# A two-layer decoder trunk on one core: three more projection pairs as split products, rotary angles on GpSimd

## The chip, the cores and the metric

The kernel runs on one core of one Trainium2 chip. The metric is device time in microseconds: 1081.44 us is the median of three runs of the kernel before (1079.23 to 1082.0).

## The reference

Two layers (D = 1024, 256 positions, batch 1) over a residual x, and a last RMSNorm. Each layer's first half, cut to what matters:

```
h = rmsnorm(x, norm1_g[l]) * (1 + sc1) + sh1          # shifts and scales from silu(c) @ w_mod
z = h @ w_in[l]                                       # one wide projection
ya = rglru_branch(...z...)                            # convolution, gated linear recurrence
yb = diff_attention(zq, zk, zv, positions, ...)       # ang = positions * inv_freq; cos, sin; partial rotary
yc = rwkv7_mix(...z...)                               # token shift, LoRA products, state recurrence
merged = sigmoid(za)*(ya@Wa) + sigmoid(zb)*(yb@Wb) + sigmoid(zc)*(yc@Wc)
x = x + gt1 * (merged @ w_out[l])
```

In `rwkv7_mix` the token shift is z_t + (z_{t-1} - z_t) * mu, and three small LoRA products give decay, `a` and gate: tanh(wd) @ w2, ad @ a2, sigmoid(gd) @ g2. The second half of a layer is a gated MLP with a short convolution. All of it is fp32, and so is the output.

## The kernel before

Everything lies in SBUF with channels on partitions: X, H and the projected tiles are 128 channels x 256 positions. The engines run five streams of instructions written out by hand; semaphores alone set their order, and each engine works its queue strictly in order.

**Pairs.** The large weights come as pairs of output tiles, 1 MB each (two halves of 128x1024), in a ring of four slots. SyncE issues pair g when pair g - 4 is done (`pair`, L500). In a layer, pair 0 is the LoRA inputs, 1 and 2 are K, 3 and 4 R, 5 and 6 V, 7 to 10 the recurrent branch (`LR` = 7), 11 to 16 the attention's q, k, v (`AT` = 11), and the gates and merges follow (`GA` = 17).

**Plain and split products.** A pair is multiplied in one of two ways. `product` (L1826) is 16 plain fp32 matmuls a pair (the trace lists each as two). `product_split` takes three reduced-width (fp32r) matmuls for each plain one: high weight x high input, high x low, low x high (`passes`, L1806 to L1808). It needs the high part of the weights, a ScalarE copy (`half_pairs_high`, L702, into WC or WCR, alternating by pair), the low part, a VectorE subtraction (`half_pairs_low`, L1198, written over the ring slot as RLO), and the same for the input: `input_high` (L688, L689, into HG0 and HG1) and `input_low` (L1212, HGL over H). HG0 lies over SW, where the first layer's LoRA weights are too. Layer 1 is split from pair 1 on; layer 0 from pair 7 (`split_from`). The first split pair of a layer does its two products on the high input first and the one on the low input after them.

**Order around the change, layer 0.** TensorE: pairs 0 to 3, the products that sum the shift of the first pairs (`shift_column`, L1814, inside pair 2, on the sums GG that VectorE accumulates at L1184 and L1187), the LoRA products for decay and `a` (L1897, waiting for ScalarE's tanh, L720 to L723), pairs 4 and 5, the LoRA gate product (L1907), pairs 6, 7, 8, the kk sums (L1926), pairs 9 and 10, the bonus sums (L1937), pairs 11 to 16. ScalarE: evacuations of each pair (`evac`, L672; L821 for pairs 11 on), the tanh block between the evacuations of pairs 2 and 3, then some derived values, the two sines (L733, L734), the LoRA tanhs (L740), and the high parts. VectorE: token shift of the LoRA inputs, two `wmod` blocks, `derived` (lambda terms, and the rotary angles L1057 to L1076: positions times frequency, then the range reduction, once for sine and once for cosine; last the sine's sign, L1101), the shift of K (L1156 to L1160), scans and shifts of R and V, and the low parts between them; from L1394 on the rotation with SIN and COS. GpSimd: memsets, the DMAs of later `wmod` blocks (L570), two kinds of additions later on, and nothing else in this stretch.

Of the kernel before, what the change touches and what calls it, by code (L numbers as in the profile page):

```python
# [23 lines left out]
I32 = mybir.dt.int32  # L24
# [134 lines left out]
FILL_ZY = 6  # L159
FILL_TURN, FILL_READ, FILL_CHAIN, FILL_STATE, FILL_OUT = 4, 8, 4, 6, 8  # L160
# [36 lines left out]
def trunk_kernel(nc, wmain, wmod, small, v1v2, params, consts, lqk, x_t, positions, y_t):  # L197
    ctx = ExitStack()
    with ctx:
# [154 lines left out]
        def split_from(l):  # L354

            return 1 if l else LR

        def lora_weights(l, a, n):

            return (R[:, 8:12, :].rearrange("p a b -> p (a b)") if l else SW)[:, a:a + n]  # L360
# [115 lines left out]
        def _(sp):  # L476
# [37 lines left out]
            for l in range(L):  # L514
# [7 lines left out]
                if l == 0:  # L522
                    sp.dma_start(lora_weights(l, WL, 1024), small[l, :, 0:1024]).then_inc(s_sw, 16)
# [34 lines left out]
        def _(pool):  # L558
# [13 lines left out]
            def add_squares(n):  # L572

                pool.wait_ge(x_sq, 8 * n + 4)
                pool.tensor_tensor(H[:, 0:2, :], H[:, 0:2, :], H[:, 2:4, :], ALU.add).then_inc(sq_add, 1)
                pool.wait_ge(sq_add, 4 * n - 3)
# [3 lines left out]
                pool.wait_ge(sq_add, 4 * n - 1)  # L580
                pool.tensor_tensor(H[:, 0, :], H[:, 0, :], H[:, 4, :], ALU.add).then_inc(sq_add, 1)

            pool.wait_ge(s_w[2], 16)
            for l in range(L):
# [7 lines left out]
                m1 = m0 + 16  # L592
                mod_blocks(m0 + 2, m1)
# [30 lines left out]
        def _(act):  # L624
# [49 lines left out]
            for l in range(L):  # L674
# [16 lines left out]
                def half_pairs_high(a, b):  # L691

                    for y in range(a, b):
                        k, m = LR + y // 2, y % 2
                        g, far = PAIRS * l + k, k >= split_from(l) + 2
                        if m == 0:
                            act.wait_ge(s_w[g % 4], 16 * (g // 4 + 1))
                        if far and m == 0:
                            act.wait_ge(p_half, (GA - LR) * l + k - 2 - split_from(l) + 1)
# [17 lines left out]
                evac(l, 2, G[:, 4:6, :])  # L717
                next_high(2)
# [7 lines left out]
                if l == 0:  # L726
# [19 lines left out]
                for b in range(2):  # L746
                    A(GG[:, 2 * b:2 * b + 2, :], duo(4 + b), ACT.Copy).then_inc(lora_act, 1)
                if l == 0:
                    input_high()
                    half_pairs_high(0, 4)  # L750
                else:
                    next_high(5)
                evac(l, 6, G[:, 12:14, :])
                if l:
                    next_high(6)
# [270 lines left out]
        def _(dve):  # L1026
# [16 lines left out]
            def derived():  # L1043
# [12 lines left out]
                ang, k1, red = YB[:, 2, :], YB[:, 3, :], RT[:, :]  # L1056
                V.tensor_copy(YB[:, 1, :], YB[:, 0, :].bitcast(I32)).then_inc(step, tick(n_step))  # L1057
                after()
                V.tensor_scalar(ang, YB[:, 1, :], C[:, FREQ:FREQ + 1], None, ALU.mult).then_inc(step, tick(n_step))
                for n, out in enumerate((red, YB[:, 1, :])):  # L1060
                    after()
                    V.tensor_scalar(k1, ang, 1.0 / SQ2PI, 0.25 * n, ALU.mult, ALU.add).then_inc(step, tick(n_step))
                    after()
                    V.tensor_scalar(k1, k1, MAGIC, None, ALU.add).then_inc(step, tick(n_step))
                    after()
                    V.tensor_scalar(k1, k1, -MAGIC, None, ALU.add).then_inc(step, tick(n_step))
                    after()
                    V.scalar_tensor_tensor(out, k1, -C1, ang, ALU.mult, ALU.add).then_inc(step, tick(n_step))
                    after()
                    V.scalar_tensor_tensor(out, k1, -C2, out, ALU.mult, ALU.add).then_inc(step, tick(n_step))  # L1070
                    after()
                    V.scalar_tensor_tensor(out, k1, -C3, out, ALU.mult, ALU.add).then_inc(step, tick(n_step))
                    after()
                    V.tensor_scalar(out, out, 0.5 * math.pi * n, PI_IN, ALU.add, ALU.min).then_inc(step, tick(n_step))
                    after()
                    V.tensor_scalar(out, out, -PI_IN, None, ALU.max).then_inc(pre_dve, 1)  # L1076
# [19 lines left out]
                V.reduce_sum(sm[:, 24:25], mat(ROT), AX_X).then_inc(step, tick(n_step))  # L1096
                after()
                V.tensor_scalar(sm[:, 24:25], sm[:, 24:25], -1.0, None, ALU.mult).then_inc(step, tick(n_step))
                after()
                dve.wait_ge(pre_act, 6)  # L1100
                V.tensor_scalar(SIN[:, :], SIN[:, :], sm[:, 24:25], None, ALU.mult).then_inc(step, tick(n_step))  # L1101
# [64 lines left out]
            for l in range(L):  # L1166
# [25 lines left out]
                def half_pairs_low(a, b):  # L1192

                    for y in range(a, b):
                        s = (PAIRS * l + LR + y // 2) % 4
                        part = slice(y % 2 * D, y % 2 * D + D)
                        dve.wait_ge(ph_ready, 2 * (GA - LR) * l + 2 * (LR - split_from(l)) + y + 1)
# [39 lines left out]
                early_low(4)  # L1237
                after()
# [4 lines left out]
                early_low(5)  # L1243
                dve.wait_ge(lora_act, 10 * l + 8)
# [34 lines left out]
                if l == 0:  # L1279
                    half_pairs_low(0, 2)  # L1280
                    input_low()
# [103 lines left out]

                for b in range(4):
# [345 lines left out]
        def _(pe):  # L1732
# [44 lines left out]
            def ones_sum(n, between=None):  # L1777
                for m in range(KT) if n == 0 else (0, 6, 7):
                    if n and m == 0:
                        pe.wait_ge(sq_add, 4 * n)  # L1780
# [54 lines left out]
            def product_split(l, k):  # L1835
# [4 lines left out]
                for m in range(2):  # L1840
                    pe.wait_ge(pl_ready, 2 * (GA - LR) * l + y1 + m + 1)
# [22 lines left out]
            for l in range(L):  # L1864
# [35 lines left out]
                for k in (4, 5):  # L1900
                    if l:
                        product_split(l, k)
                    else:
                        product(l, k, H)
# [3 lines left out]
                last.then_inc(lora_mm, 1)  # L1908
                if l:
                    product_split(l, 6)  # L1910
                    product_split(l, LR)
# [5 lines left out]
                    product_split(l, LR + 1)  # L1917
                else:
                    product(l, 6, H)
                    product_split(l, LR)  # L1920
                    product_split(l, LR + 1)
# [517 lines left out]
```

## Time and profile before

| | |
|---|---|
| median of three runs | 1081.44 us |
| the profiled execution | 1079.48 us, its span 1077.9 us |
| TensorE busy | 1055.1 us, 98% |
| VectorE busy | 849.6 us, 79% |
| ScalarE busy | 582.2 us, 54% |
| GpSimd busy | 120.0 us, 11% |
| granted TensorE clock, mean | 0.996 |

Read the busy shares as averages over many stages. What a change is worth shows in the chain that ended last and in who waits for whom in the stretch that it touches, here the first 150 us.

### The profile page before, as it was taken

Reading aid. Unit: us, or ns where it says so; the run is one execution under the profiler, and the core shown is the slowest. Engines: PE = TensorE matmul, PEld = TensorE weight load, DVE = VectorE, ACT = ScalarE, POOL = GpSimd, SP = SyncE. Lnnn points to the kernel's source line nnn. Section 1 sums busy time; section 2 is a strip of 40 time slices with the busy share of each in tenths; the row PEclk is TensorE's granted clock in tenths of the full one; section 3 lists DMA queues with packets and bytes.
Section 4 is the critical chain, followed back from the end, with each engine's and each line's share of the span. In section 5 each row is a group of like instructions: output and inputs, shape, how many; then the busy total and the mean of one; then the engine's idle time right before and its main releaser. Section 6 shows DMA issues by size and latency. Waiting matters only on the chain.

```text
span 1077.9 us, 24053 instructions
## 1 busy us (share of the span) xinstructions
PE 1055.1 (98%) x10020; PEld 965.3 (90%) x10020; DVE 849.6 (79%) x1255; ACT 582.2 (54%) x894; POOL 120.0 (11%) x138
## 2 busy tenths in 40 slices
PE   7999999999999999999999999999999999999997
PEld 6789988788798999999989999878877999999996
DVE  5798998686687889987768899978766878888763
ACT  2266567632555666663455575783328466666433
POOL 0100000056002000001120000002530200000001
PEclk9999999999999999999999999999999999999999
DMA  9956445544246566668855546451615565455651
GB/s 368 345 197 227 172 167 227 194 158 139 99 181 253 212 234 228 229 225 293 319 168 195 196 162 230 159 204 65 231 61 195 185 245 195 175 178 192 227 204 40
DMA packets 41751, 214.86 MB, mean 199 GB/s; under 512 B 8096, under 2 KB 8736, under 8 KB 22336
## 3 DMA queue, kind: packets, MB, share of 16 engines
q1 hardware_dynamic: 30144, 171.65, 43.3%
q0 software_dynamic: 11520, 41.95, 11.1%
q8 instruction: 67, 1.10, 0.4%
q14 instruction: 20, 0.16, 0.0%
HBM read 212.01 MB, written 1.05 MB: 198 GB/s over the span
## 4 chain that ended last, share of the span: by engine, by line
PE 92%; DVE 3%; DMA 3%; SPq 1%; ACT 1%; issue 1%; DVEq 0%; ACTq 0%
PE ps L1808 18%; PE ps L1806 18%; PE ps L1807 18%; PE ps L1996 6%; PE ps L2000 6%; PE ps L1994 6%; PE ps L1826 4%; PE ps L2105 3%; DMA TK<-wmod_dram 2%; DVE macc L1119 1%; PE ps L2283 1%; PE ps L1764 1%; PE ps L2096 1%; DMA mring<-wmod_dram 1%; PE ps L2021 1%; PE ps L1951 1%
## 5 line engine op out<-in xcount | busy, mean ns | idle before, releaser
L972 ACT ACTIVATE WH<-ring 128x1024 fp32r<-128x1024 f32 x144 | 151.9, 1060 | 163.9 <-PE ps L1808 155.8
L1650 DVE TENSOR_TENSOR WLO<-ring,WH 128x1024 fp32r<-128x1024 f32 x144 | 175.4, 1232 | 66.7 <-ACT WH L972 66.7
L1808 PE MATMUL ps<-HH,WLO 128*128 128x256 f32 x736 | 208.4, 283 | 0.0
L1807 PE MATMUL ps<-HL,WH 128*128 128x256 f32 x736 | 206.8, 281 | 0.0
L1806 PE MATMUL ps<-HH,WH 128*128 128x256 f32 x736 | 205.2, 279 | 0.0
L1808 PEld LDWEIGHTS ps<-HH,WLO 128*128 128x128 f32 x736 | 138.9, 189 | 0.0
L1806 PEld LDWEIGHTS ps<-HH,WH 128*128 128x128 f32 x736 | 138.7, 188 | 0.0
L1807 PEld LDWEIGHTS ps<-HL,WH 128*128 128x128 f32 x736 | 138.1, 188 | 0.0
L570 POOL DMA_DIRECT2D mring<-wmod_dram x80 | 43.2, 540 | 761.7 <-DVE macc L1119 456.0
L1119 DVE SCALAR_TENSOR_TENSOR macc<-mring,sm,macc 128x1024 f32<-128x1024 f32 x70 | 96.4, 1377 | 18.2 <-DMA mring<-wmod_dram 15.8
L1808 PE MATMUL ps<-GH,WLO 128*128 128x256 f32 x384 | 108.4, 282 | 0.0
L1806 PE MATMUL ps<-GH,WH 128*128 128x256 f32 x384 | 108.3, 282 | 0.0
L1807 PE MATMUL ps<-GL,WH 128*128 128x256 f32 x384 | 108.0, 281 | 0.0
L1808 PE MATMUL ps<-HG,RLO 128*128 128x256 f32 x384 | 108.0, 281 | 0.0
L1678 DVE SCALAR_TENSOR_TENSOR TK<-ps,PR,TK 128x255 f32<-128x255 f32 x192 | 79.1, 475 | 0.0
L2000 PE MATMUL ps<-RLO,HG 128*128 128x512 f32 x192 | 77.8, 405 | 0.0
L1808 PEld LDWEIGHTS ps<-GH,WLO 128*128 128x128 f32 x384 | 73.7, 192 | 0.0
L1808 PEld LDWEIGHTS ps<-HG,RLO 128*128 128x128 f32 x384 | 72.6, 189 | 0.0
L1807 PEld LDWEIGHTS ps<-GL,WH 128*128 128x128 f32 x384 | 72.3, 188 | 0.0
L1806 PEld LDWEIGHTS ps<-GH,WH 128*128 128x128 f32 x384 | 72.1, 188 | 0.2
L785 ACT ACTIVATE WC<-ring 128x1024 fp32r<-128x1024 f32 x36 | 37.7, 1054 | 55.0 <-PE ps L1996 31.9
L1806 PE MATMUL ps<-HG,WCR 128*128 128x256 f32 x208 | 58.9, 283 | 0.0
(404 smaller groups left out, 2499.9 us busy)
## 6 DMA issues: line engine op xcount, KB each, us to landing
ring<-wmain_dram SPq DMA_DIRECT2D x150, 1024.0 KB, 4.9
mring<-wmod_dram POOLq DMA_DIRECT2D x80, 512.0 KB, 5.1
G<-wmod_dram SPq DMA_DIRECT2D x3, 1024.0 KB, 9.3
R<-wmod_dram SPq DMA_DIRECT2D x2, 1024.0 KB, 18.2
TK<-wmod_dram SPq DMA_DIRECT2D x2, 1024.0 KB, 19.8
X<-x_t_dram SPq DMA_DIRECT2D x1, 1024.0 KB, 4.9
R<-wmod_dram SPq DMA_DIRECT2D x2, 512.0 KB, 12.2
y_dram<-H SPq DMA_DIRECT2D x4, 256.0 KB, 2.2
```

The costliest lines, as they stand in the source:

```text
L570: pool.dma_start(mring[:, n % 2, :], wmod[mod_row(n)]).then_inc(s_m[n % 2], 16)
L972: A(WH[:, n % 2, part], ring[:, b, part], ACT.Copy).then_inc(hi_ready, 1)
L1119: V.scalar_tensor_tensor(macc[:, u % 2, :], block, sm[:, CSIL + kt:CSIL + kt + 1], macc[:, u % 2, :], ALU.mult, ALU.add).then_inc(mod_used, 1)
L1650: V.tensor_tensor(WLO[:, n % 2, part], ring[:, b, part], WH[:, n % 2, part].bitcast(F32), ALU.subtract).then_inc(lo_ready, 1)
L1678: ins = V.scalar_tensor_tensor(UB[:, q % 2, t, d:S], duo(b)[:, t, 0:S - d], PR[:, l, bass.ds(j + (COL["fw"] + 48 * (2 - d)), 1)], UB[:, q ...
L1806: MM(out, w_high[:, at], high, start=start, stop=False, skip_group_check=True)
L1807: MM(out, w_high[:, at], low, start=False, stop=False, skip_group_check=True)
L1808: return MM(out, w_low[:, at], high, start=False, stop=stop, skip_group_check=True)
L1826: last = MM(ps[:, g % 4, m * S:(m + 1) * S], w_of(g, m, i), rhs[:, i, :], start=(i == 0), stop=(i == KT - 1))
L1994: MM(ps[:, b, :], high[:, tk], w_high, start=(k == 0), stop=False, skip_group_check=True)
L1996: i = MM(ps[:, b, :], low[:, tk], w_high, start=False, stop=False, skip_group_check=True)
L2000: i = MM(ps[:, b, :], high[:, tk], w_low, start=False, stop=(k == nk - 1), skip_group_check=True)
```

## The change

It does four things, all in layer 0:

1. `split_from(0)` is 4 instead of 7: pairs 4, 5 and 6 are split products. `input_high` and the high parts of pairs 4 to 8 move forward in ScalarE's queue (the first two right behind the evacuation of pair 2), and `input_low` and the low parts of pairs 4 to 7 in VectorE's (`early_low`).
2. The first layer's LoRA weights w2, a2, g2 go to R[:, 8:12], as the second layer's do, since HG0 is now written while they are in use. SyncE waits for nine used `wmod` blocks ahead of that load.
3. The rotary angles are computed by GpSimd, in 24 instructions (VectorE's fused multiply-adds become a multiply and an addition), after its memset of R and ahead of its further `wmod` DMAs. `derived` is cut in three: `derived`, `derived_mid` and `sine_signed`.
4. ScalarE takes the sines after the high parts of pair 8, and VectorE puts the sine's sign in ahead of the first rotation.

```diff
         def split_from(l):
-            return 1 if l else LR
+            return 1 if l else 4
         def lora_weights(l, a, n):
-            return (R[:, 8:12, :].rearrange("p a b -> p (a b)") if l else SW)[:, a:a + n]
+            return R[:, 8:12, :].rearrange("p a b -> p (a b)")[:, a:a + n]
...
                 if l == 0:
+                    sp.wait_ge(mod_used, added(9))
                     sp.dma_start(lora_weights(l, WL, 1024), small[l, :, 0:1024]).then_inc(s_sw, 16)
...
+            def angles():
+                pool.wait_ge(s_par, 64)
+                pool.wait_ge(h_pre, 8)
+                ang, k1, red = YB[:, 2, :], YB[:, 3, :], RT[:, :]
+                pool.tensor_copy(YB[:, 1, :], YB[:, 0, :].bitcast(I32)).then_inc(sq_add, 1)
+                pool.wait_ge(sq_add, 1)
+                pool.tensor_scalar(ang, YB[:, 1, :], C[:, FREQ:FREQ + 1], None, ALU.mult).then_inc(sq_add, 1)
+                for n, out in enumerate((red, YB[:, 1, :])):
+                    done = 2 + 11 * n
+                    pool.wait_ge(sq_add, done)
+                    pool.tensor_scalar(k1, ang, 1.0 / SQ2PI, 0.25 * n, ALU.mult, ALU.add).then_inc(sq_add, 1)
+                    pool.wait_ge(sq_add, done + 1)
+                    pool.tensor_scalar(k1, k1, MAGIC, None, ALU.add).then_inc(sq_add, 1)
+                    pool.wait_ge(sq_add, done + 2)
+                    pool.tensor_scalar(k1, k1, -MAGIC, None, ALU.add).then_inc(sq_add, 1)
+                    for i, part in enumerate((C1, C2, C3)):
+                        pool.wait_ge(sq_add, done + 3 + 2 * i)
+                        pool.tensor_scalar(COS[:, :], k1, -part, None, ALU.mult).then_inc(sq_add, 1)
+                        pool.wait_ge(sq_add, done + 4 + 2 * i)
+                        pool.tensor_tensor(out, COS[:, :], ang if i == 0 else out, ALU.add).then_inc(sq_add, 1)
+                    pool.wait_ge(sq_add, done + 9)
+                    pool.tensor_scalar(out, out, 0.5 * math.pi * n, PI_IN, ALU.add, ALU.min).then_inc(sq_add, 1)
+                    pool.wait_ge(sq_add, done + 10)
+                    pool.tensor_scalar(out, out, -PI_IN, None, ALU.max).then_inc(sq_add, 1)
...
                 def next_high(k):
-                    if l:
+                    if k + 2 >= split_from(l):
                         half_pairs_high(2 * (k + 2 - LR), 2 * (k + 3 - LR))
...
                 evac(l, 2, G[:, 4:6, :])
+                if l == 0:
+                    input_high()
                 next_high(2)
                 act.wait_ge(lora_z, 2 * l + 2)
                 A(YA[0:64, 0, :], YA[0:64, 0, :], ACT.Tanh).then_inc(lora_t, 1)
...
-                    act.wait_ge(pre_dve, 5)
-                    A(SIN[:, :], RT[:, :], ACT.Sin).then_inc(pre_act, 1)
-                    A(COS[:, :], YB[:, 1, :], ACT.Sin).then_inc(pre_act, 1)
...
+                next_high(5)
+                evac(l, 6, G[:, 12:14, :])
+                next_high(6)
                 if l == 0:
-                    input_high()
-                    half_pairs_high(0, 4)
+                    act.wait_ge(sq_add, TRIG)
+                    A(SIN[:, :], RT[:, :], ACT.Sin).then_inc(pre_act, 1)
+                    A(COS[:, :], YB[:, 1, :], ACT.Sin).then_inc(pre_act, 1)
...
                 def early_low(k):
-                    if l:
+                    if k >= split_from(l):
                         half_pairs_low(2 * (k - LR), 2 * (k + 1 - LR))
...
                 shift(G[:, 2:6, :], K_, 4, l, 2)
                 early_low(4)
+                if l == 0:
+                    input_low()
...
                 early_low(5)
+                if l == 0:
+                    derived_mid()
...
                 if l == 0:
-                    half_pairs_low(0, 2)
-                    input_low()
                     half_pairs_low(2, 4)
...
+                if l == 0:
+                    sine_signed()
                 for b in range(4):
...
                 for k in (4, 5):
-                    if l:
-                        product_split(l, k)
-                    else:
-                        product(l, k, H)
+                    product_split(l, k)
```

The angle instructions that `derived` loses (L1057 to L1076), and the counts of the semaphores that go with the longer list of split pairs, are left out here.

## Rows read from the trace of the kernel before

**Rows 1.** The page's first part: busy us, share of the span, instructions.
```profile
PE 1055.1 (98%) x10020; PEld 965.3 (90%) x10020; DVE 849.6 (79%) x1255; ACT 582.2 (54%) x894; POOL 120.0 (11%) x138
```

**Rows 2.** The chain that ended last, 38 to 150 us: start, us, what.
```profile
45.82 0.79 PE ps L1814 x8
46.60 7.45 PE ps L1826 x34
...
56.94 14.01 PE ps L1826 x64
...
72.68 6.91 PE ps L1826 x32
```

**Rows 3.** ScalarE's timeline: start, us, what, idle before and its releaser.
```profile
48.97 1.28 ACT L720 ACT_TABLE_LOAD   x1
...
51.02 0.42 ACT L723 ACTIVATE YA<-YA 128x256 f32<-128x256 f32 x1
...
75.58 2.00 ACT L702 ACTIVATE WC<-ring 128x1024 fp32r<-128x1024 f32 x2
...
122.82 0.60 ACT L821 ACTIVATE R<-ps 128x512 f32<-128x512 f32 x1 [3.20 <-PE ps L1808]
...
128.50 0.60 ACT L821 ACTIVATE R<-ps 128x512 f32<-128x512 f32 x1 [3.18 <-PE ps L1808]
```

**Rows 4.** The tile `ring`, 46 to 52 us: loads of pairs 4 to 6.
```profile
L500 SPq DMA_DIRECT2D ring<-wmain_dram x3: 430/430/513, 47.0 to 48.0; - x3
...
DMA to landing us min/median/max: 5.0/7.7/11.0
```

**Rows 5.** The load of the positions (line L491).
```profile
L491 SPq DMA_DIRECT2D YB<-positions_dram x1: 1710/1710/1710, 24.5 to 24.5; - x1
...
DMA to landing us min/median/max: 14.9/14.9/14.9
```

**Rows 6.** VectorE's timeline, 38 to 130 us.
```profile
39.37 5.47 DVE L1187 SCALAR_TENSOR_TENSOR GG<-ring,mod,GG 128x512 f32<-128x512 f32 x7
...
47.77 0.69 DVE L1156 TENSOR_TENSOR YA<-G 128x510 f32<-128x510 f32 x1 [0.96 <-ACT G L682]
...
52.56 0.29 DVE L1057 CAST YB<-YB 128x256 f32<-128x256 int32 x1
...
59.07 0.15 DVE L1081 TENSOR_TENSOR sm<-sm 128x1 f32<-128x1 f32 x1
...
61.28 0.36 DVE L1101 TENSOR_SCALAR SIN<-SIN,sm 128x256 f32<-128x256 f32 x1
...
64.72 1.14 DVE L1240 TENSOR_SCALAR KK<-ZS,PR 128x256 f32<-128x256 f32 x4
...
76.74 2.36 DVE L1198 TENSOR_TENSOR RLO<-ring,WC 128x1024 fp32r<-128x1024 f32 x2 [0.32 <-ACT WC L702]
79.63 2.36 DVE L1212 TENSOR_TENSOR HGL<-H,HG 128x1024 fp32r<-128x1024 f32 x2 [0.53 <-PE ps L1826]
81.91 2.35 DVE L1198 TENSOR_TENSOR RLO<-ring,WCR 128x1024 fp32r<-128x1024 f32 x2
84.17 1.22 DVE L1156 TENSOR_TENSOR ZS<-G 128x1020 f32<-128x1020 f32 x1
...
105.76 1.29 DVE L1322 TENSOR_TENSOR BON<-ps,ZS 128x512 f32<-128x512 f32 x2 [0.75 <-PE ps L1937]
...
126.52 2.35 DVE L1198 TENSOR_TENSOR RLO<-ring,WC 128x1024 fp32r<-128x1024 f32 x2
```

**Rows 7.** GpSimd's instructions by form: count, busy us, mean ns, idle before.
```profile
L581 POOL TENSOR_TENSOR H<-H 128x256 f32<-128x256 f32 x4 | 2.9, 734 | 0.3
...
L559 POOL MEMSET SW<- 128x1024 f32 x1 | 1.0, 951 | 0.3 <-POOLq L2432 0.3
```

**Rows 8.** Timelines of GpSimd and VectorE, 326 to 336 us.
```profile
330.13 1.75 POOL L577 TENSOR_TENSOR H<-H 128x256 f32<-128x256 f32 x1
...
330.06 2.91 DVE L1650 TENSOR_TENSOR WLO<-ring,WH 128x1024 fp32r<-128x1024 f32 x2 [0.37 <-ACT WH L972]
```

More of the change, by code:

```diff
@@ L159 @@
 FILL_ZY = 6
+TRIG = 24
 FILL_TURN, FILL_READ, FILL_CHAIN, FILL_STATE, FILL_OUT = 4, 8, 4, 6, 8
@@ L575, in add_squares @@
                 pool.tensor_tensor(H[:, 0:2, :], H[:, 0:2, :], H[:, 2:4, :], ALU.add).then_inc(sq_add, 1)
-                pool.wait_ge(sq_add, 4 * n - 3)
+                pool.wait_ge(sq_add, TRIG + 4 * n - 3)
                 pool.tensor_tensor(H[:, 0, :], H[:, 0, :], H[:, 1, :], ALU.add).then_inc(sq_add, 1)
@@ L579, in add_squares @@
                 pool.tensor_tensor(H[:, 4, :], H[:, 4, :], H[:, 5, :], ALU.add).then_inc(sq_add, 1)
-                pool.wait_ge(sq_add, 4 * n - 1)
+                pool.wait_ge(sq_add, TRIG + 4 * n - 1)
                 pool.tensor_tensor(H[:, 0, :], H[:, 0, :], H[:, 4, :], ALU.add).then_inc(sq_add, 1)
+            def angles():
[22 more added lines that the diff above has]
+                    pool.tensor_scalar(out, out, -PI_IN, None, ALU.max).then_inc(sq_add, 1)
             pool.wait_ge(s_w[2], 16)
@@ L592, in _ @@
                 m1 = m0 + 16
+                if l == 0:
+                    angles()
                 mod_blocks(m0 + 2, m1)
@@ L698, in half_pairs_high @@
                         if far and m == 0:
-                            act.wait_ge(p_half, (GA - LR) * l + k - 2 - split_from(l) + 1)
+                            act.wait_ge(p_half, (GA - split_from(0)) * l + k - 2 - split_from(l) + 1)
                         elif far:
@@ L1055, in derived, with derived_mid @@
                 V.scalar_tensor_tensor(CEN[:, :], mat(BLOCKS), -1.0 / 64, mat(IDENT), ALU.mult, ALU.add).then_inc(cen_ready, 1)
[L1056 to L1076, printed above, removed]
+            def derived_mid():
                 dve.wait_ge(pre_act, 4)
@@ L1095, in derived, with sine_signed @@
                 after()
-                V.reduce_sum(sm[:, 24:25], mat(ROT), AX_X).then_inc(step, tick(n_step))
+                V.reduce_sum(sm[:, CSH:CSH + 1], mat(ROT), AX_X).then_inc(step, tick(n_step))
                 after()
-                V.tensor_scalar(sm[:, 24:25], sm[:, 24:25], -1.0, None, ALU.mult).then_inc(step, tick(n_step))
+                V.tensor_scalar(sm[:, CSH:CSH + 1], sm[:, CSH:CSH + 1], -1.0, None, ALU.mult).then_inc(step, tick(n_step))
+            def sine_signed():
                 after()
                 dve.wait_ge(pre_act, 6)
-                V.tensor_scalar(SIN[:, :], SIN[:, :], sm[:, 24:25], None, ALU.mult).then_inc(step, tick(n_step))
+                V.tensor_scalar(SIN[:, :], SIN[:, :], sm[:, CSH:CSH + 1], None, ALU.mult).then_inc(step, tick(n_step))
                 after()
@@ L1196, in half_pairs_low @@
                         part = slice(y % 2 * D, y % 2 * D + D)
-                        dve.wait_ge(ph_ready, 2 * (GA - LR) * l + 2 * (LR - split_from(l)) + y + 1)
+                        dve.wait_ge(ph_ready, 2 * (GA - split_from(0)) * l + 2 * (LR - split_from(l)) + y + 1)
                         V.tensor_tensor(RLO[:, s, part], ring[:, s, part], half_high(y).bitcast(F32), ALU.subtract).then_inc(pl_ready, 1)
                 def early_low(k):
-                    if l:
+                    if k >= split_from(l):
                         half_pairs_low(2 * (k - LR), 2 * (k + 1 - LR))
@@ L1384, in dve_chunks @@
                         weights_low(x)
+                if l == 0:
+                    sine_signed()
                 for b in range(4):
@@ L1779, in ones_sum @@
                     if n and m == 0:
-                        pe.wait_ge(sq_add, 4 * n)
+                        pe.wait_ge(sq_add, TRIG + 4 * n)
                     else:
@@ L1840, in product_split @@
                 for m in range(2):
-                    pe.wait_ge(pl_ready, 2 * (GA - LR) * l + y1 + m + 1)
+                    pe.wait_ge(pl_ready, 2 * (GA - split_from(0)) * l + y1 + m + 1)
                     out, wh, wl = ps[:, g % 4, m * S:(m + 1) * S], half_high(y0 + m), RLO[:, g % 4, m * D:m * D + D]
@@ L1900, in _ @@
                 for k in (4, 5):
-                    if l:
-                        product_split(l, k)
-                    else:
-                        product(l, k, H)
+                    product_split(l, k)
                 pe.wait_ge(lora_act, 10 * l + 4)
@@ L1908, in _ @@
                 last.then_inc(lora_mm, 1)
+                product_split(l, 6)
+                product_split(l, LR)
                 if l:
-                    product_split(l, 6)
-                    product_split(l, LR)
                     pe.wait_ge(lora_act, 10 * l + 8)
@@ L1916, in _ @@
                     last.then_inc(zv_up, 1)
[L1917 to L1921, printed above, removed]
+                product_split(l, LR + 1)
                 pe.wait_ge(kk_sq, l + 1)
```

3 lines of the change are left out of this document (removed).

## The prediction

> **What bounds the kernel now.** I read the page first: TensorE is busy for 98% of the span [rows 1], so a change pays only through TensorE's own work or its waits. Next, the chain that ended last, from 46 to 80 us [rows 2]: it lies on TensorE alone. Pair 3 ends at 54.05; pairs 4 and 5, as plain fp32 products, take 14.01 us together, pair 6 takes 6.91. The reader is to see that nothing else is on that chain there. Then ScalarE's timeline [rows 3]: pairs 13 and 14 are split products, and their evacuations start 5.68 us apart, so a split pair costs 5.68 us. Last, VectorE's timeline [rows 6]: it runs the low parts of the weights just ahead of TensorE. The low part of pair 15 starts at 126.52, its first half (half of 2.35 us) is there at 127.7, and TensorE takes pair 15 shortly before 128.50, when the evacuation of pair 14 begins [rows 3]. I take 0.6 us of room (0.8 at most). VectorE is the second bound.
>
> **The change, part by part.**
> *Pairs 4 to 6 split.* TensorE's work falls by 14.01 + 6.91 - 3 x 5.68 = 3.9 us.
>
> *ScalarE ahead of the LoRA tanh.* `input_high` (two copies) and the high parts of pair 4 (two more) now stand in ScalarE's queue before the tanh that TensorE's LoRA products wait for. A copy of that shape takes 1.0 us (two take 2.00) [rows 3]. The tanh's table load began at 48.97; after `input_high` ScalarE is free at 50.9, but pair 4 isn't there: it is issued at 47.0 and the quickest of the three issues needs 5.0 us [rows 4], so 52.0. Two copies to 54.0, then the old stretch from table load to the last copy, 51.44 - 48.97 = 2.5 us [rows 3]: 56.4. TensorE is there at 54.05 and loses 2.4 us. Behind it wait the evacuation of pair 3 and all later ones. Net for TensorE alone: 3.9 - 2.4 = 1.5 us gained.
>
> *LoRA weights in R[8:12].* One load moves in its destination only. SyncE issues it after a wait for nine blocks, which VectorE finishes before SyncE comes to that point; what is queued behind it, the other small weights, the masks and pair 4, isn't held. Cost 0.
>
> *Low parts and derived vectors on VectorE.* The old way from the angles' first instruction to the shift of V is 52.56 to 84.17. Out go the angles, 52.56 to 59.07, 6.5 us, the sine's sign (0.36, with its wait 0.4) and two idle gaps of 0.32 and 0.53, which were waits for ScalarE's late high parts and for pair 6 [rows 6]. In come three more pairs of low parts at 84.17 - 81.91 = 2.26 us, 6.8 us. Sum -6.5 - 0.4 - 0.85 + 6.8 = -1.0: without anything else VectorE would come to the shift of V 1.0 us earlier. It wins another 0.75 at the bonus, where it waited for TensorE, and gives 0.4 back where the sine's sign now stands, ahead of the first rotation [rows 6].
>
> *Angles on GpSimd.* 24 instructions on 128x256: 18 with one input tensor, 6 with two. They begin at 24.5 + 14.9 = 39.4, when the positions land [rows 5]. The sines are wanted by ScalarE only at about 80, so their own length costs nothing, nor does the delay of the `wmod` blocks queued behind them on GpSimd (used from 91 us). But GpSimd and VectorE hold each other up: at 330.06 two VectorE instructions with both inputs in SBUF take 2.91 us beside GpSimd additions [rows 8], against 2.35 for two of the same form and shape at 81.91 with GpSimd idle [rows 6]. In between ran one 128x256 addition of GpSimd, which took 1.75 us instead of its 0.73 [rows 7, 8]. So one two-input instruction of GpSimd costs VectorE 0.55 us, and they take turns. The one-input instruction isn't in this trace. Below, a memset of 128x1024 takes 0.95 [rows 7], a quarter of it 0.24; above, the two-input 0.55. I take 0.3, about half of the two-input one, since it reads half as much.
>
> How much of this is covered: VectorE's seven accumulations end at 39.37 + 5.47 = 44.84 [rows 6], and TensorE's product on their result starts at 45.82 [rows 2], so they may be about 0.8 us late with a signal's way kept. They take turns with six one-input instructions, 6 x 0.3 = 1.8 us: 1.0 uncovered, for TensorE at 46 and for VectorE behind it (TensorE gives it back, since the tanh stays at 56.4). While VectorE then waits for that product and for ScalarE (0.8 us and the 0.96 us before 47.77 [rows 2, 6]), three more fit, two of them two-input. Fifteen are left: 4 x 0.55 + 11 x 0.3 = 5.5 us, all before the shift of K ends, in a stretch where VectorE has no idle time. The delay in all, call it C, is 1.0 + 5.5 = 6.5. Ends: C = 0 if they don't hold each other up here; with 0.55 for all, 6 x 0.55 - 0.8 + 15 x 0.55 = 10.8.
>
> The Trainium skill (SBUF — State Buffer, Who interferes with whom) says that a VectorE instruction with two SBUF inputs, or in a two-port mode, and a GpSimd instruction that reads SBUF exclude each other for the whole instruction. By that rule, the trace agrees with its 0.55 us, all 24 instructions exclude VectorE. The skill (GPSIMD Engine Reference, Engine selection) calls GpSimd's one-input work roughly line rate; by VectorE's 0.96 GHz an estimate of 0.27 us for 256 columns, and C would be 6.0; no row here shows such an instruction.
>
> *The sum.* TensorE is ready for pair 4 at 56.4 plus the LoRA products, 56.94 - 54.05 = 2.9 [rows 2], 59.3. VectorE begins the shift of K at 52.56 instead of 61.67 (the sine's sign and 0.03); it takes until 64.72, 3.05 us [rows 6], half a low part 1.13, so 56.7 without C and about 63 with it. TensorE waits 3.9 us there, and doesn't get ahead again: by its own work it would start pair 8 at 59.3 + 4 x 5.68 + the gate products, 72.68 - (56.94 + 14.01) = 1.7 [rows 2], 83.7; the first half of that pair's low part stands 2.26 - 1.13 before the shift of V, 83.2 - 1.1 + 6.5 = 88.6. What remains at pair 15 is VectorE's lateness less the room: C - 1.0 - 0.75 + 0.4 - 0.6 = C - 1.95. With C = 6.5 that is +4.55 us. After it TensorE is ahead of nothing that would give it back: the scores' operands come with about 1.9 us of room, and from there TensorE is the bound. The profiled execution took 1079.48 us, so 1084.0; it stands 1.96 under the median of the runs, 1081.44, and the prediction is made on that: 1086.0.
>
> **Rivals.**
> *The two engines don't get in each other's way here* (C near 0, or under 1.95). TensorE's own sum decides: 1.5 us gained, 1079.9, not slower. For it: three quarters of GpSimd's instructions have one input, and the row that prices the conflict is of two inputs on both sides. Against: 1.75 for 0.73. It decides while C is under about 0.5; the sign turns at C = 1.95.
> *One-input instructions cost as much as two-input ones.* C = 10.8, +8.85 us, 1090.3; the accumulations would be 2.5 us late for TensorE's product at 46.
> *The tanh isn't late and VectorE keeps ahead.* Then 3.9 us of TensorE's work would come free; VectorE's lead limits it to 1.95, 1079.5. A gain of over 0.3% (3.2 us) needs both bounds to be wrong. ScalarE's queue order speaks against it.
> *Pair 4 lands later than 52.0* (the third of the three needs 11.0 us [rows 4]). Up to 3.9 us more are hidden by the wait for VectorE in my case; where C is near 0, 3 us more are a loss of 1.5 net, 1082.9: within no change.
>
> **Numbers.** Forecast case 0.5 (one-input price between 0.2 and 0.4: C from 4.8 to 8.2, +2.9 to +6.2). No conflict 0.25, with the late pair 4 in it. Full price 0.18. Clear gain 0.07. The range reaches from VectorE's bound on a gain, 1079.5, to the full price, 1090.3. 0.3%, about what a measurement can tell from no change, is 3.2 us; of the forecast case about 0.45 of 0.5 lies above it. Slower 0.45 + 0.18 = 0.63, same 0.25 + 0.05 = 0.3, faster 0.07.
>
> **What the profile after would show.** GpSimd's angle instructions at about 0.45 us each (hold and issue), from 39.4 to about 60, and stretched beside VectorE; VectorE's accumulations in GG, its shift of K and its first low parts lengthened by about 7 us together, some 0.8 of it without effect; the LoRA products at 56.4 instead of 54; TensorE idle for some 4 us before pair 4, with VectorE's RLO as releaser, and again by some tenths before pairs 5 to 8 and 15; the shift of V at about 89.7. If instead that shift starts near 83 and TensorE's only new gap is the 2.4 us at 54, the conflict was mis-sized and the time is near 1080. If GpSimd's one-input instructions take 0.7 us alone, the upper rival holds.

## The result, and the profile of the changed kernel

The changed kernel took 1087.54 us (median of 5 runs, 1085.92 to 1089.09) against 1081.44 us: 6.1 us slower, ratio 1.0063 with a 95% interval of 1.0048 to 1.0078. The forecast was 1086.0 us, slower. The profiled execution took 1087.13 us, its span is 1085.3 us, 7.4 us over that of before. The sign and most of the size came out, but in the trace only 2.3 of these 7.4 us arose where the forecast put the loss; the rest has another cause. One run of e1 below, 1149.24 us at a granted clock of 0.85, is a slow one and is left out of its figures.

The page's first part, after; before is [rows 1]:

```profile
PE 1052.5 (97%) x10068; PEld 963.1 (89%) x10068; DVE 854.6 (79%) x1243; ACT 589.2 (54%) x900; POOL 146.1 (13%) x162
```

TensorE has 48 matmuls more (three pairs of 48 in place of 32) and 2.6 us less work. GpSimd's busy time grew by 26 us for the 24 angle instructions; at the shortest time of each form, given below, they would take 18 x 0.40 + 6 x 0.73 = 11.6 us.

ScalarE's timeline, after (the copies ahead of the tanh) [rows 3]:

```profile
49.32 1.08 ACT L718 ACTIVATE HG<-H 128x1024 fp32r<-128x1024 f32 x1
50.27 1.08 ACT L719 ACTIVATE HG<-H 128x1024 fp32r<-128x1024 f32 x1
51.81 2.01 ACT L732 ACTIVATE WCR<-ring 128x1024 fp32r<-128x1024 f32 x2 [0.46 <-DMA ring<-wmain_dram]
53.84 1.28 ACT L752 ACT_TABLE_LOAD   x1
...
55.89 0.42 ACT L755 ACTIVATE YA<-YA 128x256 f32<-128x256 f32 x1
```

The last tanh copy ends at 56.3, and the LoRA products start at 56.51; the forecast said 56.4. TensorE's waits from 50 to 100 us, after:

```profile
PE ps L1824 <- DVE RLO L1212: 2.0, 2, 1.3
PE ps L1915 <- issue: 2.0, 1, 2.0
```

The second line is the wait for the tanh. The first is the wait for low parts, ahead of pairs 5 and 6. GpSimd's angle instructions by form, after (count, busy us, mean ns, idle before):

```profile
L603 POOL TENSOR_SCALAR COS<-YB 128x256 f32<-128x256 f32 x6 | 7.4, 1234 | 0.5
L605 POOL TENSOR_TENSOR YB<-COS,YB 128x256 f32<-128x256 f32 x3 | 3.0, 1003 | 0.3
...
L609 POOL TENSOR_SCALAR YB<-YB 128x256 f32<-128x256 f32 x1 | 1.9, 1902 | 0.1
```

The shortest one-input instruction takes 0.40 us and the shortest two-input one 0.73; beside VectorE most of them stretch to between 0.85 and 1.9 (1.09 on the mean of all 24). VectorE's timeline, after [rows 6]:

```profile
39.46 6.54 DVE L1201 SCALAR_TENSOR_TENSOR GG<-ring,mod,GG 128x512 f32<-128x512 f32 x7
...
57.28 3.09 DVE L1212 TENSOR_TENSOR RLO<-ring,WCR 128x1024 fp32r<-128x1024 f32 x2
60.30 3.09 DVE L1226 TENSOR_TENSOR HGL<-H,HG 128x1024 fp32r<-128x1024 f32 x2
63.31 1.99 DVE L1256 TENSOR_SCALAR KK<-ZS,PR 128x256 f32<-128x256 f32 x4
...
87.28 1.21 DVE L1170 TENSOR_TENSOR ZS<-G 128x1020 f32<-128x1020 f32 x1
```

The accumulations take 6.54 us for 5.47, a low part 3.09 for 2.35, KK 1.99 for 1.13: the two engines do hold each other up. The shift of V starts at 87.28. Without conflict the forecast had it at 83.2, so C, the delay by the conflict, is 4.1 us and not 6.5.

How late is each kernel at fixed points of the program? The table takes the start of the same VectorE instruction in each trace, less its start before. The first column is the scores, where the changed stage ends. Each row is one execution, set against one of the kernel before (1079.48 us, near the fastest of its runs), so a row says where time goes; what it is worth is told by the medians.

| profiled execution | 147.12 (scores) | 215.73 | 240.71 | 540.60 | 785.49 (layer 1) | 998.82 |
|---|---|---|---|---|---|---|
| after | +2.32 | +3.47 | +4.59 | +6.05 | +5.94 | +7.23 |
| only angles (e2) | +0.46 | -0.04 | +0.15 | +1.48 | +1.66 | +1.71 |
| tanh first, no angles (e7) | -1.99 | -1.06 | +0.01 | +1.37 | +1.25 | +2.57 |
| before, 48 matmuls more (e9) | +1.44 | +2.65 | +3.62 | +4.61 | +4.22 | +5.54 |
| after, 128 matmuls more (e11) | +2.04 | +1.62 | +2.14 | +2.29 | +2.29 | +2.29 |
| e7, 128 matmuls more (e10) | -2.31 | -2.73 | -2.21 | -2.01 | -2.13 | -2.17 |
| only pair 6 split (e12) | -0.79 | +1.67 | +2.10 | +3.31 | +3.42 | +3.44 |

("128 more" counts the 48 of the split pairs and 80 that do no work.) The changed stage costs 2.3 us. Another 3.7 us come between the scores and 541 us and 1.3 near 795 us, where the change has altered nothing. That part was the question for the experiments.

### The profile page after: what moved, and what is told of

It is laid out like the page before. It is cut to its first block, busy times and chain, and to the rows that moved or that the text cites. A ratio compares the mean times of both kernels' runs of the same rounds, so it can differ in the third digit from the quotient of the medians.

```text
span 1085.3 us, 24172 instructions
## 1 busy us (share of the span) xinstructions
PE 1052.5 (97%) x10068; PEld 963.1 (89%) x10068; DVE 854.6 (79%) x1243; ACT 589.2 (54%) x900; POOL 146.1 (13%) x162
## 4 chain that ended last, share of the span: by engine, by line
PE 79%; DVE 12%; DMA 4%; issue 2%; ACT 1%; SPq 1%; DVEq 0%; ACTq 0%
PE ps L1826 17%; PE ps L1824 16%; PE ps L1825 16%; PE ps L2007 5%; PE ps L2011 5%; PE ps L2005 5%; DVE RLO L1212 2%; DMA mring<-wmod_dram 2%; PE ps L2116 2%; DMA TK<-wmod_dram 2%; DVE macc L1133 2%; PE ps L2294 1%; PE ps L2107 1%; PE ps L1782 1%; PE ps L2032 1%
## 5 line engine op out<-in xcount | busy, mean ns | idle before, releaser
L1826 PE MATMUL ps<-HG,RLO 128*128 128x256 f32 x432 | 121.4, 281 | 0.0
L1133 DVE SCALAR_TENSOR_TENSOR macc<-mring,sm,macc 128x1024 f32<-128x1024 f32 x70 | 96.6, 1380 | 13.3 <-DMA mring<-wmod_dram 11.6
L1826 PEld LDWEIGHTS ps<-HG,RLO 128*128 128x128 f32 x432 | 81.6, 189 | 0.0
L1824 PE MATMUL ps<-HG,WCR 128*128 128x256 f32 x224 | 63.5, 283 | 0.7 <-DVE RLO L1212 0.7
## 6 DMA issues: line engine op xcount, KB each, us to landing
R<-wmod_dram SPq DMA_DIRECT2D x2, 512.0 KB, 12.4
```

What stands on the lines that cost most here:

```text
L1133: V.scalar_tensor_tensor(macc[:, u % 2, :], block, sm[:, CSIL + kt:CSIL + kt + 1], macc[:, u % 2, :], ALU.mult, ALU.add).then_inc(mod_used, 1)
L1824: MM(out, w_high[:, at], high, start=start, stop=False, skip_group_check=True)
L1826: return MM(out, w_low[:, at], high, start=False, stop=stop, skip_group_check=True)
```

## Experiments

### First four: which part of the change costs what

**e1_no_angles** (after, without the 24 instructions on GpSimd):

```diff
-                pool.tensor_copy(YB[:, 1, :], YB[:, 0, :].bitcast(I32)).then_inc(sq_add, 1)
...
+                pool.memset(RT[:, :], 0.5).then_inc(sq_add, 1)
+                pool.memset(YB[:, 1, :], 0.5).then_inc(sq_add, 1)
```

> The changed kernel with the 24 angle instructions of GpSimd left out; two memsets of their outputs stand in their place, so the rotation is by a constant angle, and nobody computes the angles. Theory of the prediction (GpSimd and VectorE exclude each other): VectorE's accumulations end at 44.9 again, its shift of V starts at 83.2 instead of 87.3, TensorE's only new gap is the one of about 2 us ahead of the LoRA products, and the scores' first products come at about 144.5 (before 146.0, changed 148.3). If everything behind the scores follows, the time is near 1080. Rival (the further 5 us that the changed kernel loses behind 150 us come from something of their own, such as loads or the place of instructions): the scores at 144.5, but the time near 1084 to 1085. Rival that the conflict is harmless: shift of V at 87, time near 1087.

Measured 1085.36 us (median of eleven runs, 1082.17 to 1088.64), ratio 1.0040 [1.0026, 1.0055]. VectorE came through undelayed (accumulations 5.48 us, `AB` at 65.60), as forecast for no conflict, and yet the kernel stayed 4.6 us over the kernel before. So the conflict isn't the whole loss. The scores were 1.64 us late, where 1.5 us early had been expected, and the trace shows why the first stage gained so little. Stretches of it (busy us of PE, PEld, DVE, ACT, POOL, then the granted clock):

```profile
54.00:56.00 2.00, 0.21 (x1) 0.00 (x0) 1.97 (x6) 1.96 (x5) 0.00 (x0) 1.00 0.99 416
56.00:58.00 2.00, 1.92 (x8) 1.72 (x10) 2.00 (x3) 2.00 (x3) 0.00 (x0) 0.68 1.03 424
58.00:60.00 2.00, 2.00 (x9) 1.64 (x7) 2.00 (x3) 1.97 (x5) 0.00 (x0) 0.50 1.03 426
60.00:62.00 2.00, 2.00 (x7) 1.33 (x6) 2.00 (x6) 1.97 (x4) 0.00 (x0) 0.50 0.30 123
62.00:64.00 2.00, 2.00 (x13) 2.00 (x12) 1.95 (x6) 2.00 (x7) 0.00 (x0) 0.61 0.03 8
```

TensorE idles for the tanh from 54.2 to 56.1, and then its granted clock is 0.50 (1.2 instead of 2.4 GHz) until 63.6, which the 0.61 of the last stretch gives; the LoRA products took 4.99 us instead of 2.94. In the profiled execution of after the same wait was there and the clock stayed at 1.00.

**e2_only_angles** (before, with the angles on GpSimd and the sines taken later; pairs 4 to 6 plain):

```diff
-            return 1 if l else 4
+            return 1 if l else LR
```

> The kernel before with the angles alone on GpSimd and the sines and the sine's sign taken later, as in the changed kernel; pairs 4 to 6 stay plain products. Theory: VectorE loses 6.5 us of work and gets back about 5 us of waiting, and up to pair 7 TensorE doesn't wait for low parts, so only the accumulations' lateness of some 0.3 us shows: 1081 to 1082, no change. Rival (GpSimd's work itself costs what the change lost): near 1086.

1080.73 us, ratio 1.0003 [0.9992, 1.0014]: no change. The scores were 0.46 us late in its trace, about the 0.3 us expected from the accumulations. The 6.5 us of angles that VectorE gets rid of pay for the rest of the conflict: its shift of K began at 59.73, and at 61.67 in the kernel before.

**e3_tanh_first** (after, the tanh block ahead of `input_high` and of the high parts of pair 4):

```diff
-                if l == 0:
-                    input_high()
-                next_high(2)
...
                 A(YA[:, 1, :], YA[:, 1, :], ACT.Copy, scale=0.5, bias=0.5).then_inc(lora_t, 1)
+                if l == 0:
+                    input_high()
+                    next_high(2)
```

> The changed kernel with ScalarE's tanh block put back ahead of the copies of the input and of pair 4. Theory: TensorE's LoRA products start at 54.4 instead of 56.3, but it then waits for VectorE's low part of pair 4 (58.9) all the same: time as the changed kernel within 0.5 us. Rival (the late tanh is what costs): 2 us less, 1085.5.

1087.54 us, ratio 1.0061 [1.0048, 1.0074]: as after. The wait for the tanh turned into a wait for pair 4's low part (TensorE busy for 0.56 and 1.19 us of the two stretches 58 to 60 and 60 to 62), and after it the granted clock was 0.59 and 0.56 until 66. The scores were 2.9 us late, but that isn't the edit's alone: in this execution the granted clock was at 0.50 from 38.5 to 41.9 as well, ahead of all that the edit touches, and TensorE's products on the accumulations began 1.2 us later than in after.

**e4_angles_vector** (after, with the angles back on VectorE):

```diff
-                if l == 0:
-                    angles()
...
+                V.tensor_copy(YB[:, 1, :], YB[:, 0, :].bitcast(I32)).then_inc(step, tick(n_step))
```

> The changed kernel with the angles back on VectorE at their old place (16 fused instructions and two more, 6.5 us), the sines still late. Theory: VectorE reaches the shift of V at 83.2 + 6.5 = 89.7 instead of 87.3, and TensorE is later by the same 2.4 us: near 1089.5 to 1090. Rival (the moving of the angles to GpSimd is what makes the change slow): faster than the changed kernel, 1083 or less.

1089.74 us, ratio 1.0085 [1.0072, 1.0098], as expected: with the angles on VectorE 2.2 us more are lost than with the conflict. How the time is lost is not what the expectation says. VectorE's shift of V began at 89.16 (89.7 expected), but TensorE's two waits stand further ahead, for the tanh and then for pair 4's low part:

```profile
55.79 4.72 PE L1908 MATMUL ps<-YA,R 64*128 64x256 f32 x16 [1.90 <-issue]
63.15 0.55 PE L1859 MATMUL ps<-HG,WCR 128*128 128x256 f32 x1 [2.64 <-issue]
```

Between and behind them the granted clock is 0.50 from 56.7 to 67.0, and from there to the scores TensorE waits for VectorE no more. How much of the 2.2 us is VectorE's lateness and how much the clock isn't separated.

### The loss behind 150 us

In all four runs with split pairs the lateness grew by 2.5 to 3.9 us from the scores to 541 us. The first step of it is at 168 us: a chunk of gate weights was waited for, and ScalarE idled 2.50 us for it instead of 1.11. The issues of that load with the time to landing, before and after:

```profile
ring<-wmain_dram SPq DMA_DIRECT2D x1, 1024.0 KB, 7.0
```

```profile
ring<-wmain_dram SPq DMA_DIRECT2D x1, 1024.0 KB, 8.4
```

It is the second of two loads of 1 MB that are issued back to back, at 160.1 before and at 162.3 after. Nothing of the kernel's own is in flight beside them. But the queues of the trace have another row there. After, 167.5 to 168.0 and then 169.5 to 170.0 us (queue, packets, MB, share of 16 DMA engines):

```profile
q1 hardware_dynamic: 23, 0.18, 85.1%
q8 instruction: 1, 0.02, 12.4%
...
q1 hardware_dynamic: 1, 0.01, 3.9%
```

A block of instructions was fetched while the ring load ran. It held one DMA engine for about 1.0 us (12.4% of 16 x 0.5 us), and the last packets of the load came in singly behind it, until 170.0; ScalarE began its copy at 170.50. In the kernel before, the fetch came at 176.25, when the next load ran whose late landing (8.3 us) held up nobody. Whose instructions are they? The windows from the start to the moment of the fetch, before and then after (the first count is TensorE's matmuls):

```profile
0.00:176.25 176.25, 167.87 (x1096) 149.18 (x1097) 147.51 (x234) 91.56 (x144) 7.83 (x21) 0.99 0.66 246
```

```profile
0.00:167.50 167.50, 153.49 (x1097) 138.06 (x1098) 143.25 (x206) 91.27 (x144) 34.00 (x45) 1.00 0.68 247
```

1096 and 1097 matmuls: the fetch follows TensorE's count, and in the kernel before its two neighbours stand 125 matmuls ahead of it and 128 behind it. The 48 matmuls of the split pairs bring it forward by 48 matmuls of work, into the load. The Trainium skill (Runtime: NRT & Kernel Launch, Instruction fetch mechanics) says that each engine's sequencer fetches blocks of 256 instructions over a DMA queue of its own, mostly hidden; the trace agrees with the block (128 matmuls and as many weight loads), and the landing of 8.4 us shows what is not hidden.

This gives theory A, that the position of TensorE's instruction blocks costs the time. Theory B was that the loss comes from how late the engines enter the stretch. To tell them apart, e5, e6 and e8 added small products of 128x32 that no one reads; the trace counts them as 48 matmuls in e5 and 80 in e6 and e8. e7 has none, and neither e7 nor e8 computes the angles.

```diff
+            def small_products(n):
+                for _ in range(n):
+                    MM(ps[:, 5, 0:32], ones[:, :], X[:, 0, 0:32], start=True, stop=True, skip_group_check=True)
...
                     keep_clock(4, 5, X[:, 0, :])
+                    small_products(24)
```

> The kernel before with 24 small products (128x32, their result is never read) in a stretch where TensorE idles for 1.65 us at about 16.6 us, and nothing else. They give TensorE 48 more matmul instructions, as many as the split pairs 4 to 6 add, and no later work. Theory A (where TensorE's next block of instructions is fetched moves with the number of its instructions; in the profile of after it falls into the load of a ring slot at 167 us, which lands 8.4 us after its issue instead of 7.0): the time grows by 2 to 4 us behind 160 us, to about 1084, with the fetch at 166 to 168 us and the same late load. Theory B (the loss behind 150 us comes from how late VectorE and TensorE enter that stretch): no change, within 0.5 us of 1081.

> The kernel after with 40 such small products in two idle stretches of TensorE (24 at 16.6 us, 16 at 37 us). With the 48 of the split pairs that is 128 matmuls, one whole block of instructions, so the fetches behind 80 us stand again where those of before stand. Theory A: the load at 162 us lands 7.0 us after its issue, the growth of the lateness behind 150 us (about 5 us) shrinks by 2 to 4 us, and the time is about 1084.5. Theory B: 1087.5 as after.

> After with the LoRA tanh ahead of the high parts of pair 4 and without the 24 angle instructions (two memsets of 128x256 stand for them, so the rotary part is not computed). Neither the wait for the tanh nor the wait for VectorE ahead of pair 4 is left. If the fall of TensorE's clock to half (0.50 in the run without angles) follows such a wait, the clock stays at 1.00 and VectorE's lead alone sets the stretch to 150 us: 1 to 2 us ahead of before at the scores instead of 1.6 us behind. With theory A the part behind 150 us still loses 3 to 4 us: 1082 to 1083. With theory B it loses nothing: 1079.5.

> The kernel of the run e7 with the 40 small products of e6. Theory A: faster than e7 by 2 to 4 us, about 1079.5, the best that split pairs 4 to 6 can give here. Theory B: as e7.

| run | us, ratio | late at scores | at 240.71 | at 540.60 |
|---|---|---|---|---|
| e5 | 1086.87, 1.0049 [1.0033, 1.0065] | +2.97 | +4.73 | +6.24 |
| e6 | 1088.28, 1.0064 [1.0044, 1.0084] | +6.63 | +6.59 | +7.90 |
| e7 | 1082.61, 1.0014 [1.0001, 1.0026] | -1.99 | +0.01 | +1.37 |
| e8 | 1087.49, 1.0047 [1.0030, 1.0065] | +4.12 | +5.06 | +7.08 |

As a comparison of times e5, e6 and e8 missed: the small products took 0.14 us each, 6.8 us for 48 where 1.65 us were idle, and the granted clock was at 0.50 for 6.8 us beside and behind them, so that TensorE came 3 us late to the products on the accumulations in e5 and 6 us in e6 and e8, and neither theory's time could be read off. e8 also speaks against theory A as the whole story: with its count padded it lost nothing at 168 us, but 3.0 us from the scores to 541 us. e7, which has no padding, came as theory A expected: it has neither wait, its clock stayed at 1.00 from 50 to 150 us, it was 2.0 us ahead at the scores, and it still lost 3.4 us behind them.

e9, e10 and e11 took the cheapest product of the kernel's own shapes, 64x64 at 36 ns a pass, in the same idle stretches.

```diff
-                    MM(ps[:, 5, 0:32], ones[:, :], X[:, 0, 0:32], start=True, stop=True, skip_group_check=True)
+                    MM(ps[0:64, 5, 0:SUM], ones[:, 0:64], ones[:, 0:SUM], start=True, stop=True, skip_group_check=True)
```

> As e5, but the 24 extra products are of the cheapest shape in this kernel (64x64, 36 ns a pass), 1.7 us in all, in the idle 1.65 us at 16.6 us; so TensorE gets the same 48 matmul instructions and isn't made late, as it was by 3 us in e5. Theory A (position of the instruction fetches): on time to 160 us, the load issued at 159 us lands after 8.3 us instead of 7.0, the lateness grows to 2 to 3.5 us by 540 us, time 1083 to 1085. Theory B (the growth in e5 came from its late start): no change, 1081.

1084.89 us, ratio 1.0044 [1.0029, 1.0059]. Only TensorE's count of instructions is changed, in idle time, and the kernel before becomes 4.0 us slower. The added products didn't make TensorE late; a later piece of its work, before and in e9:

```profile
36.98 1.15 PE L1764 MATMUL ps<-ones,macc 128*64 128x64 f32 x32 [1.73 <-DVE macc L1119]
```

```profile
36.85 1.15 PE L1764 MATMUL ps<-ones,macc 128*64 128x64 f32 x32 [1.72 <-DVE macc L1119]
```

In the profiled execution, which ended 5.5 us later than that of before, the granted clock then fell to 0.50 from 38.1 to 41.5, and TensorE lost 1.4 us there, ahead of the scores; 3.2 us came from the scores to 541 us, and 1.3 near 795. The fetch and the load, in two answers:

```profile
0.00:166.50 166.50, 159.08 (x1096) 142.62 (x1097) 137.64 (x218) 85.16 (x137) 7.83 (x21) 0.99 0.68 247
```

```profile
ring<-wmain_dram SPq DMA_DIRECT2D x1, 1024.0 KB, 8.4
```

> The kernel of e7 (tanh first, rotary angles not computed) with 40 such cheap products (24 in the idle stretch at 16.6 us, 16 in that at 37 us), in place of the dear ones of e8. Fetches where those of before are, no late start. Theory A: e7 less about 2 us, 1080 to 1081. Theory B: as e7, 1082.6.

1079.56 us, ratio 0.9991 [0.9982, 1.0000], 3.05 us less than e7; lateness from -2.31 at the scores to -2.13 at 785 us, so the growth is gone.

> The kernel after with the same 40 cheap products, in place of the dear ones of e6. Theory A: after less about 2 us, 1085.5; what is left over before is then the conflict of GpSimd and VectorE, the late tanh, and what is still unexplained behind 240 us. Theory B: 1087.5.

1085.11 us, ratio 1.0044 [1.0029, 1.0059], 2.4 us less than after. In the trace the lateness is +2.04 at the scores and +2.29 at 785 us: the growth is gone here too. Its fetch and its load:

```profile
0.00:177.25 177.25, 167.52 (x1220) 150.44 (x1221) 152.04 (x219) 96.50 (x149) 33.97 (x45) 1.00 0.67 242
```

```profile
ring<-wmain_dram SPq DMA_DIRECT2D x1, 1024.0 KB, 6.8
```

The fetch stands at 1220 matmuls, one block (1096 + 128, within some records), and in the time of the kernel it stands where that of before stood, at 177 us. The five runs of e11 scatter from 1082.21 to 1086.98, and the profiled one is the fastest, so the median is over what the trace explains; the intervals of the ratios of after and e11 overlap. The trace and the pair e7 and e10, whose intervals just don't overlap, carry the point.

**e12_split_6_only** (after, with pairs 4 and 5 plain):

```diff
-            return 1 if l else 4
+            return 1 if l else 6
...
                 for k in (4, 5):
-                    product_split(l, k)
+                    if l == 0:
+                        product(0, k, H)
+                    else:
+                        product_split(l, k)
```

(`input_high` moves behind the evacuation of pair 4 with it, and `input_low` to just ahead of the low part of pair 7.)

> After, but only pair 6 is a split product; pairs 4 and 5 are plain again, so the LoRA tanh has nothing new ahead of it on ScalarE. The angles stay on GpSimd. TensorE gains 6.91 - 5.68 = 1.2 us, VectorE loses one low part (2.3 us) of what the angles gave it. It has 16 more matmuls than before, which moves the fetch at 176 us to about 173 us, still behind the load issued at 159 us. Theory A: 1079.5 to 1081, the time of before or a little less. If the loss behind 150 us comes with any split pair whatever the number of instructions: 1083 or more.

1082.26 us, ratio 1.0010 [1.0001, 1.0018], over the 1081 at most that was expected. At the scores it was 0.79 us ahead, as the two costs say. Then the fetch, moved by 16 more matmuls, fell at 169.75 us (not at 173, as worked out), where the loads of 169.6 to 170.4 us are issued. The later of them, in its trace:

```profile
ring<-wmain_dram SPq DMA_DIRECT2D x1, 1024.0 KB, 9.3
```

The expectation had looked at one load only (that of 159 us, which landed after 7.0). The kernel lost 2.5 us by 216 us and 4.1 by 541. Its version with padding that puts the fetches back was not run. No kernel that computes everything beat the kernel before.

### The steps, in all fourteen traces

Set side by side, the traces say how far theory A reaches. The second column is the second load at 160 us, from issue to landing; the others are the growth of TensorE's lateness over a step, in us.

| kernels | load | at 168 us | near 266 us | near 795 us |
|---|---|---|---|---|
| before | 6.98 | | | |
| 48 matmuls more: after, e1, e3, e4, e5, e7, e9 | 8.24 to 8.38 | 0.7 to 0.9 | 1.2 | 1.2 to 1.3 |
| none more: e2 | 6.82 | -0.1 | 1.2 | 0.0 |
| 128 more: e6, e8 | 6.89, 6.91 | 0.0 | 1.2 | 0.0 |
| 128 more: e10, e11 | 6.87, 6.81 | 0.0 | 0.0 | 0.0 |
| 16 more: e12 | 7.01 (the next two 7.22, 9.25) | 2.4 | 1.2 | 0.0 |

The step at 168 us and the one near 795 us follow the count in every trace, however late a kernel comes; only the first of them was traced to a load. The one near 266 us doesn't: e2 has it with the count of before. Since e2's median is that of before all the same, it may be a step that executions of any of these kernels take or don't. One more step, between 236 and 255 us, takes any size from 0 to 1.6 us and doesn't follow the count either.

## Why the prediction was right, and where it was right by luck

*Pairs 4 to 6 split, TensorE's work.* The gain is real: with both waits gone and the fetches in place (e10), TensorE reaches the scores 2.3 us early. The forecast bounded that by VectorE's lead at 1.95 us. (e10 doesn't compute the angles.)

*ScalarE ahead of the tanh.* Right: pair 4 was waited for until 51.81 (forecast 52.0), the products began at 56.51 (56.4). What the forecast didn't see is that such a wait can cost more than its length: in e1, e3 and e4 the granted clock fell to half after it.

*LoRA weights' buffer, 0.* Nothing in the traces speaks against it; it was not tried alone.

*VectorE without conflict.* `AB` began at 65.60 in e1, after 65.7 by the forecast's working.

*The conflict, C = 6.5.* This term was mis-sized. C is 4.1 (shift of V at 87.28, not 89.7); between e10 and e11 the low part of pair 8 is 4.4 us later. The price of 0.3 us for a one-input instruction was too high: the accumulations lost 1.07 us against five of these and one two-input instruction, 0.18 each on the mean. That the two engines hold each other up came out, for one-input instructions too; that they shut each other out for a whole instruction isn't shown, since 0.18 us is less than half of the shortest one. The formula C - 1.95 holds well: it gives 2.15 with the measured C, and the scores were 2.32 us late. The way there is the forecast's too: behind pair 8 TensorE was 1.4 us late by its own waits, and VectorE's lateness made it 2.3 by pair 15.

*TensorE waits 3.9 us ahead of pair 4.* This failed. It waited for nothing there: the first half of that low part was there at 57.28 + 1.54 = 58.8, before the LoRA products ended at 59.4. That is 2.1 us behind the 56.7 without conflict; only the part of C that had fallen by then counts. The forecast had all 24 instructions done by about 60; they took 1.09 us each instead of 0.45 and ended at 67.1. The waits came ahead of pairs 5 and 6 (2.0 us in all).

*"From there TensorE is the bound", so nothing is added behind the scores.* This step failed. 3.7 us were added by 541 us and 1.3 near 795. The position of TensorE's instruction fetches is shown as the cause of the step at 168 us (0.86 us of TensorE's lateness in after); the step near 795 us (1.26) follows the count in every trace, though it was not traced to a load. For the rest it is shown only that it is gone when the fetches are put back: e9 brings the growth (3.2 us by 541) into the kernel before without changing any useful work, and e10 and e11 take it away (0.3 and 0.25 us left); but e2, e6 and e8, whose fetches near 170 us stand well, lose 1.0, 1.3 and 3.0 us there. The forecast of 1086.0 was near by luck: C was 2.4 us too large, and this loss was missing. Between the profiled executions, without the 1.96 us that set the forecast on the median, it was 3.1 us short (1084.0 against 1087.13).

Of the rivals, "no conflict" (1079.9) is nearly what e10 shows, 1079.56, and it takes the tanh moved and the fetches put back to get there. "One-input as costly as two-input" fell.

Open: the first collision, at 167 us, was traced packet by packet; the later steps were not. In e2 the one near 266 us is a wait of 1.59 us for VectorE's `TK` at 269.68. What releases the 3.0 us of e8, which enters 6.4 us later than e10 and is the same kernel but for the padding's shape, isn't known; how late the engines come (theory B) may have a part in it. Why the clock fell after the wait in e1, e3 and e4, and not in the profiled executions of after and e11, isn't settled; it may be part of the scatter of these kernels' runs.

## What to carry to other kernels

When a change adds or removes many instructions on the busiest engine, compare the lateness at fixed points far behind the change. If it grows where nothing was edited, look at the instruction rows of the DMA queues beside the tightest loads, and try the kernel before with as many idle instructions added: an edit's own worth can be read only with the fetches in the same place. Here their place alone moved one kernel by 3.05 us (e7 against e10), half of what the whole edit cost. Read the granted clock beside each lateness: 1.4 us of e9's came from 3.4 us at half clock. And removing one of two waits in a row shows little if the other takes its place: the tanh's order alone (e3) gave nothing, the angles alone (e1) 0.7 us at the scores, and both together 4.3 (e7 against after).

## What the runs showed of the hardware

- TensorE's instructions came in fetches of 16 KB. Around 160 us they stood 125 and 128 matmuls apart with their weight loads, at nearly the same count (1096 or 1097, in e12 1087) in kernels of different length, and each held one DMA engine for about 1.0 us. A 1 MB load beside such a fetch landed after 8.24 to 8.38 us in seven traces, the same load without it after 6.81 to 7.01 in seven; in e12 the next one took 9.3.
- After an idle wait of TensorE of about 2 us the granted clock was 0.50 (1.2 GHz) for 6.8 us in e1, 3.4 in e3 and 10.2 in e4; after the same wait it stayed at 1.00 in after and e11.
- GpSimd's one-input 128x256 instruction took 0.40 us at best, its two-input one 0.73, and up to 1.90 us beside VectorE. VectorE's accumulations lost about 0.18 us to each of the six that ran beside them; an instruction with one input lost time too (KK, 1.99 for 1.13 us).
